# A two-block transformer stack on one core: the delta rule's triangular inverse by blocks of 16, and a reordered mixer

## What is computed

```
u = h @ w_in                       # q, k, v, z, b, a, sb_q, sb_k, sb_v, gate_a, gate_b
q, k, v = silu(conv4(q, k, v));  q, k = l2norm(q), l2norm(k)
beta = sigmoid(b);  g = -exp(a_log) * softplus(a + dt_bias)
o_a = gated_delta_rule(q, k, v, g, beta)          # 8 heads of 128
y_a = (rmsnorm(o_a) * silu(z)) @ w_branch_a
y_b = stick_breaking_attention(rmsnorm(sb_q), rmsnorm(sb_k), sb_v) @ w_branch_b
x  += (sigmoid(gate_a) * y_a + sigmoid(gate_b) * y_b) @ w_out
```

## Time and profile before

| | |
|---|---|
| median of 3 runs (lowest, highest) | 2795.54 us (2795.33, 2796.51) |
| the profiled execution's own time | 2795.47 us |
| span of its trace, first to last instruction | 2793.7 us |
| PE busy | 2540.9 us, 91% of the span |
| PE weight loads, beside it | 2360.2 us, 84% |
| DVE, ACT, POOL busy | 1538.1, 1404.1, 278.4 us |
| mean granted PE clock | 0.965 of full speed |
| DMA | 387.76 MB, mean 139 GB/s |

### The profile page before, as it was taken

The page is one execution under the profiler, slowest core; times in us unless marked ns, Lnnn a source line. Parts: engine busy times, 40 slices in busy tenths (PEclk is TensorE's granted clock), DMA queues, the critical chain, the costliest instruction groups (busy, mean ns, idle before and its releaser), DMA issues.

```text
span 2793.7 us, 46572 instructions
## 1 busy us (share of the span) xinstructions
PE 2540.9 (91%) x17917; PEld 2360.2 (84%) x17917; DVE 1538.1 (55%) x1836; ACT 1404.1 (50%) x1867; POOL 278.4 (10%) x469
## 2 busy tenths in 40 slices
PE   4999987899999899998689999989979998998998
PEld 4998876798899799887689889978878987887897
DVE  3554556445555555465554555547665544857554
ACT  3544766245545454476624545544554435455443
POOL 0000111730000000001272000000021001003000
PEclk9999998899999999999899999999999999999999
DMA  6554433014455455343301445643335564334553
GB/s 173 182 189 126 151 115 112 16 31 154 149 189 187 141 190 182 122 154 115 109 1 57 155 153 192 204 136 122 106 123 164 181 198 137 121 107 135 164 182 128
DMA packets 313158, 387.76 MB, mean 139 GB/s; under 512 B 10780, under 2 KB 288296, under 8 KB 313000
## 3 DMA queue, kind: packets, MB, share of 16 engines
q1 hardware_dynamic: 311664, 383.98, 42.5%
q10 hardware_dynamic: 1336, 1.67, 0.5%
HBM read 383.00 MB, written 2.62 MB: 138 GB/s over the span
## 4 chain that ended last, share of the span: by engine, by line
PE 69%; issue 9%; ACT 8%; DVE 7%; POOL 5%; DMA 1%; ACTq 0%; DVEq 0%; POOLq 0%; SPq 0%
PE bank L253 21%; PE bank L254 20%; PE bank L255 20%; ACT whi L239 4%; POOL arena L1218 3%; DVE wlo L245 2%; DMA raw<-in_ffn_w_in 1%; PE bank L333 1%; DVE arena L1760 1%; PE bank L611 1%; POOL arena L1203 1%; ACT arena L1657 1%; ACT arena L1639 0%; PE bank L936 0%; POOL arena L1208 0%
## 5 line engine op out<-in xcount | busy, mean ns | idle before, releaser
L245 DVE TENSOR_TENSOR wlo<-raw,whi 128x2048 fp32r<-128x2048 f32 x360 | 830.2, 2307 | 521.1 <-ACT whi L239 517.0
L253 PE MATMUL bank<-xhi,whi 128*128 128x256 f32 x3712 | 1070.3, 288 | 40.0 <-DVE arena L450 19.8
L254 PE MATMUL bank<-xlo,whi 128*128 128x256 f32 x3712 | 1056.0, 284 | 0.0
L255 PE MATMUL bank<-xhi,wlo 128*128 128x256 f32 x3712 | 1055.7, 284 | 0.0
L253 PEld LDWEIGHTS bank<-xhi,whi 128*128 128x128 f32 x3712 | 718.4, 194 | 55.7 <-issue 36.8
L239 ACT ACTIVATE whi<-raw 128x2048 fp32r<-128x2048 f32 x360 | 682.0, 1904 | 125.9 <-PE bank L255 101.5
L254 PEld LDWEIGHTS bank<-xlo,whi 128*128 128x128 f32 x3712 | 718.3, 193 | 5.3 <-issue 2.4
L255 PEld LDWEIGHTS bank<-xhi,wlo 128*128 128x128 f32 x3712 | 717.7, 193 | 0.0
L253 PE MATMUL bank<-whi,yhi 128*128 128x512 f32 x608 | 238.1, 392 | 9.3 <-DVE ylo L454 6.1
L254 PE MATMUL bank<-wlo,yhi 128*128 128x512 f32 x608 | 237.5, 391 | 0.0
L255 PE MATMUL bank<-whi,ylo 128*128 128x512 f32 x608 | 236.6, 389 | 0.0
(11 more groups left out here) (363 smaller groups left out, 3242.7 us busy)
## 6 DMA issues: line engine op xcount, KB each, us to landing
raw<-in_w_in SPq DMA_DIRECT2D x92, 1024.0 KB, 5.2
raw<-in_ffn_w_in SPq DMA_DIRECT2D x88, 1024.0 KB, 5.1
raw<-in_ffn_w_out SPq DMA_DIRECT2D x44, 1024.0 KB, 5.0
raw<-in_w_gate SPq DMA_DIRECT2D x32, 1024.0 KB, 5.4
raw<-in_w_up SPq DMA_DIRECT2D x32, 1024.0 KB, 5.4
raw<-in_w_down SPq DMA_DIRECT2D x32, 1024.0 KB, 5.1
raw<-in_w_branch_b SPq DMA_DIRECT2D x8, 1024.0 KB, 5.1
raw<-in_w_branch_a SPq DMA_DIRECT2D x8, 1024.0 KB, 5.1
```

The source lines that it names most:

```text
L245: e.tensor_tensor(wlo[s][:], raw[s][:], whi[s][:].bitcast(F32), ALU.subtract).then_inc(lo_done[s], 1)
L253: e.matmul(o, ahi, bhi, start=start, stop=False, skip_group_check=True)
L254: e.matmul(o, ahi, blo, start=False, stop=False, skip_group_check=True)
L255: return e.matmul(o, alo, bhi, start=False, stop=stop, skip_group_check=True)
```

## The change

The low four levels of the inverse (blocks of 1 to 16) are replaced. A mask "below" keeps the strictly lower part of the 128 diagonal blocks of 16x16 (16 matrices, 8 blocks each); 16 small matmuls gather them so that each partition holds one block; DVE inverts all 128 blocks at once by forward substitution along the free axis (`blocks_dve`, 29 dependent instructions on at most 240 elements, most on 56 or fewer), spreads the result, and 16 matmuls with two sets of copies and 16 more bring it back. Levels 4, 5 and 6 stay, with the mask moved from POOL ahead of the first product to DVE behind it, and with subtractions on packed halves. The gate and branch products of pairs 0 and 1 are issued inside the delta part, with the splits of units 31 to 34. All pairs alternate between two pairs of PSUM banks (4, 5 and 6, 7). The delta part no longer waits for the last silu, and POOL's spreading of g is gone (a broadcast operand of PE). In the loop over the 28 units silu's and the softplus' steps go ahead of the copy and of the taps, the attention heads take 4 turns and not 7, with two banks for the sums and two for the output, and b and a are made as 16 rows of 256 and then transposed (24 matmuls and 2 transposes). Two clearing products are gone.

```diff
+LOW = 4
+BLK = 1 << LOW
+    parts["below"] = (r // BLK == c // BLK) & (r > c)
+    parts["row_of"] = r % BLK == b[None, :]
+    parts["block_of"] = r % (P // BLK) == np.arange(P // BLK)[None, :]
-        HEAD_AT = (7, 9, 12, 14, 16, 18, 21, 23)
+        HEAD_AT = (6, 8, 11, 13, 15, 17, 20, 22)
@@ mix1_pe @@
-            norm_pe(e, j)
+            norm_pe(e, j, False)
-            mix1_delta_pe(e, l)
-            for n in range(PAIRS):
...
+            mix1_delta_pe(e, l, r0, u0)
+            for n in range(2, PAIRS):
+                pair_gate_pe(e, l, r0, u0, n)
+                pair_branch_pe(e, l, r0, u0, n)
+        def pair_gate_pe(e, l, r0, u0, n):
+            if n < 2:
+                e.wait_ge(*V["l_done"](l, 2 * n))
+            elif n < 4:
+                e.wait_ge(*V["od_r"](l, 2 * n - 4))
+            else:
+                e.wait_ge(*V["p_scaled"](l, n - 2))
+            feature_product(e, unit(r0, u0 + N1 + 2 * n), gate_bank(n), xhi, xlo)
@@ mix1_act, iteration n (the silu of n-1 ahead of the copy of n) @@
+                if head_at(n, 1) is not None:
+                    stick_softplus_act(e, l, head_at(n, 1))
+                if n - 1 in SILU:
+                    m = SILU.index(n - 1)
...
+                    e.activation(sg[m % 2], sg[m % 2], ACT.Ln, bias=one).then_inc(V["s_ln"].sem, 1)
+                if head_at(n, 3) is not None:
+                    stick_keep_act(e, l, head_at(n, 3))
@@ mix1_dve, iteration n (s_min of n-1 ahead of the taps of n) @@
+                if n - 1 in SILU:
+                    m = SILU.index(n - 1)
+                    e.wait_ge(*V["s_ln"](l, m))
+                    e.scalar_tensor_tensor(sg[m % 2], home(n - 1), 0.0, sg[m % 2], ALU.min, ALU.subtract)\
+                     .then_inc(V["s_min"].sem, 1)
@@ mix1_delta_pe @@
             e.wait_ge(*V["o_lo"](l, HEADS - 1))
-            e.wait_ge(*V["silu"](l, len(SILU) - 1))
             e.wait_ge(*V["normed"](l, len(NORM) - 1))
+            e.wait_ge(*V["pre_copied"](l, len(CONV) - 1))
...
+            pair_gate_pe(e, l, r0, u0, 0)
+            e.wait_ge(*V["m_ready"](l, GROUPS - 1))
+            e.wait_ge(*V["attn_done"](l, 0))
+            for c in range(BLK):
+                mm = e.matmul(bank[0][:, c * BLK:(c + 1) * BLK], M_blocks[:, :, c], const("row_of"), start=True, stop=True)
+            mm.then_inc(V["gathered"].sem, 1)
+            pair_branch_pe(e, l, r0, u0, 0)
+            pair_gate_pe(e, l, r0, u0, 1)
+            for b in range(4):
+                e.wait_ge(*V["spread"](l, b))
...
+                for i in range(4):
+                    mm = e.matmul(b4(b)[:, i, :], Ub[b][:, i, :], ident, start=True, stop=True)
+                mm.then_inc(V["scattered"].sem, 1)
+            pair_branch_pe(e, l, r0, u0, 1)
...
+            for g in range(GROUPS):
+                for i in range(4):
+                    mm = e.matmul(b4(g)[:, i, :], Tb[g][:, i, :], ident, start=True, stop=True)
+                mm.then_inc(V["tu_product"].sem, 1)
+            for s in range(LOW, LEVELS):
                 for g in range(GROUPS):
+                    e.wait_ge(*V["tu_done"](l, (s - LOW) * 4 + g))
+                    for i in range(4):
+                        mm = e.matmul(b4(g)[:, i, :], Lb[g][:, i, :], Ub[g][:, i, :], start=True, stop=True)
+                    mm.then_inc(V["m_product"].sem, 1)
+                for g in range(GROUPS):
+                    e.wait_ge(*V["w_kept"](l, (s - LOW) * 4 + g))
+                    for i in range(4):
+                        mm = e.matmul(halves(b4(g)[:, i, 0:64], s, False), Tb[g][:, i, :],
+                                      halves(Mb[g][:, i, :], s, True)[:, :, 1, :], start=True, stop=True)
...
@@ mix1_delta_act, behind the decay factors @@
+            split_hi(e, unit(r0, u0 + N1 + 3))
+            pair_gate_act(e, l, r0, u0, 0)
+            e.wait_ge(*V["gathered"](l))
+            e.activation(small_l, bank[0][:, 0:256], ACT.Copy).then_inc(V["l_compact"].sem, 1)
...
@@ mix1_delta_dve @@
                 up.then_inc(V["l_done"].sem, 1)
+            split_lo(e, unit(r0, u0 + N1 + 3))
+            for g in range(GROUPS):
                 e.wait_ge(*V["a_mask"](l, g))
                 e.wait_ge(*V["qk"](l, g))
                 e.tensor_tensor(flat(Ab[g]), bank[g][:], flat(Ab[g]), ALU.mult).then_inc(V["attn_done"].sem, 1)
+            pair_min_dve(e, l, 0)
+            blocks_dve(e, l)
+            pair_scaled_dve(e, l, r0, u0, 0)
+            split_lo(e, unit(r0, u0 + N1 + 4))
+            pair_min_dve(e, l, 1)
+            for b in (0, 1):
+                e.wait_ge(*V["scattered"](l, b))
+                e.tensor_copy(T_blocks[:, :, 4 * b:4 * b + 4], b4(b).rearrange("p c k -> p k c"))\
+                 .then_inc(V["t_kept_v"].sem, 1)
+            pair_scaled_dve(e, l, r0, u0, 1)
+            for g in range(GROUPS):
+                e.wait_ge(*V["tu_product"](l, g))
+                e.tensor_copy(flat(Ub[g]), bank[g][:]).then_inc(V["tu_done"].sem, 1)
+            for s in range(LOW, LEVELS):
+                mask = const(f"level{s}").unsqueeze(1).to_broadcast([P, 4, P])
+                for g in range(GROUPS):
+                    e.wait_ge(*V["m_product"](l, (s - LOW) * 4 + g))
+                    e.tensor_tensor(Mb[g], b4(g), mask, ALU.mult).then_inc(V["w_kept"].sem, 1)
+                for g in range(GROUPS):
+                    e.wait_ge(*V["tu_product"](l, (s - LOW) * 4 + 4 + g))
+                    if s < LEVELS - 1:
+                        t = pairs(Tb[g], s)[:, :, :, 0, :]
+                        e.tensor_tensor(t, t, packed(b4(4 + g), s), ALU.subtract)
+                    u = pairs(Ub[g], s)[:, :, :, 1, :]
+                    e.tensor_tensor(u, u, packed(b4(g), s), ALU.subtract).then_inc(V["tu_done"].sem, 1)
+                if s < LEVELS - 1:
+                    split_lo(e, unit(r0, u0 + N1 + 1 + s))
+        def blocks_dve(e, l):
...
+            e.tensor_tensor(small_t, const("eye"), small_l, ALU.subtract).then_inc(V["t_first"].sem, 1)
+            e.wait_ge(*V["t_first"](l))
+            for j in range(1, BLK - 1):
...
+                e.tensor_tensor(o, L[:, j:j + 1, j + 1:BLK].to_broadcast(shape), Tc[:, 0:j, j:j + 1].to_broadcast(shape),
+                                ALU.mult).then_inc(V["t_outer"].sem, 1)
+                e.wait_ge(*V["t_outer"](l, j - 1))
+                e.tensor_tensor(Tc[:, 0:j, j + 1:BLK], Tc[:, 0:j, j + 1:BLK], o, ALU.subtract).then_inc(V["t_step"].sem, 1)
```

More of the change, by code:

```diff
@@ L602, in mix1_pe @@
                         feature_product(e, unit(r0, u0 + n), bank[n % 2], xhi, xlo)
-                if n == 2:
+                if n == 1:
+                    e.wait_ge(*V["ba_copied"](l))
+                    e.sem_inc(tensor_waited)
+                    for t in range(TT):
+                        mm = e.transpose(bank[4][:, t * 16:(t + 1) * 16], ba_turn[:, t * P:(t + 1) * P], ident[0:16, 0:16])
+                    mm.then_inc(V["ba_turned"].sem, 1)
+                if n == 4:
                     e.wait_ge(*V["g_done"](l))
@@ L641, in kept_unit, with gate_bank, branch_out_bank @@
+        def gate_bank(n):
+            return bank[4 + n % 2 * 2]
+        def branch_out_bank(n):
+            return bank[5 + n % 2 * 2]
         def kept_unit(e, l, n):
@@ L672, in mix1_act @@
                     split_hi(e, unit(r0, u0 + n + 2))
-                if n == 3:
+                if n == 0:
+                    e.wait_ge(*V["ba_product"](l))
+                    e.activation(ba_turn, bank[4][0:16, 0:T], ACT.Copy).then_inc(V["ba_copied"].sem, 1)
+                if head_at(n, 1) is not None:
+                    stick_softplus_act(e, l, head_at(n, 1))
+                if n - 1 in SILU:
+                    m = SILU.index(n - 1)
+                    if n - 1 in CONV:
+                        e.wait_ge(*V["tap"](l, CONV.index(n - 1) * 4 + 3))
+                    else:
+                        e.wait_ge(*V["kept"](l, PLAIN.index(n - 1)))
+                    if m >= 2:
+                        e.wait_ge(*V["silu"](l, m - 2))
+                    e.activation(sg[m % 2], home(n - 1), ACT.Abs).then_inc(V["s_abs"].sem, 1)
+                    e.wait_ge(*V["s_abs"](l, m))
+                    e.activation(sg[m % 2], sg[m % 2], ACT.Exp, scale=-1.0).then_inc(V["s_exp"].sem, 1)
+                    e.wait_ge(*V["s_exp"](l, m))
+                    e.activation(sg[m % 2], sg[m % 2], ACT.Ln, bias=one).then_inc(V["s_ln"].sem, 1)
+                if head_at(n, 3) is not None:
+                    stick_keep_act(e, l, head_at(n, 3))
+                if n == 5:
                     small_act_2(e, l)
@@ L963, in stick_keep_act @@
             e.wait_ge(*V["o_product"](l, g))
-            e.activation(yhi[:, g, :], bank[7][:, 0:256], ACT.Copy).then_inc(V["o_hi"].sem, 1)
+            e.activation(yhi[:, g, :], bank[6 + g % 2][:, 0:256], ACT.Copy).then_inc(V["o_hi"].sem, 1)
         def stick_softplus_dve(e, l, h):
@@ L1090, in flat, with pairs, packed @@
```

(8 more changed lines are left out.)

330 lines of the change are left out of this document (155 added, 175 removed).

## The result

The changed kernel takes 2666.9 us (median of 4 runs, 2666.75 to 2667.26), the kernel before beside it 2796.0: the ratio is 0.954, with a 95% interval of 0.952 to 0.956. The forecast was 2662 us in a range of 2630 to 2715. The profiled execution after took 2666.87 us with a span of 2664.9, which is 128.8 less than the span before.

A forecast was written before the change was run, and what follows sets the result against it. PE, busy 91% of the span, bounds the kernel, so gains come from its idle or slow time or removed work. 2.9 + 10 + 20.2 + 33.5 = 66.6 us a layer, twice 133, takes 2795.5 to 2662 us; range 2630 to 2715.

The forecast's parts named there:

- b and a: 2.9 us: Products for b and a in each layer's mixer: 24 fewer at 0.12 us each save 2.9 us.
- The loop: 10 us: Loop over 28 units: gain 10 us a layer, ends 0 and 30; units 17 to 27 take 77 plus 2, against 89.6.
- Rival 1: In the loop, ACT takes the ring's place, so no gain there: 2682 us; chance 0.15.
- the ring: ACT and DVE waiting on each other in the loop's late units: 9.33 us a turn where PE needs 5.76 to 8.
- From unit 27 to gate 2: 112.3 us: Delta part, from the end of unit 27 to gate 2: 112.3 us instead of 132.5, saving 20.2 a layer.
- The costly order: DVE's low split of unit 31 ahead of the attention products: about 9 us of DVE waiting, PE idle 5.
- the lower end: Levels 4 to 6: if 64 columns cost half, DVE's 8.4 us would bind, 6.6 us less in all.
- Rival 2: The clock falls within the levels, whose 28.4 us double at half clock: 2719 us; chance 0.10.
- The pairs: 69.1 us: Six pairs behind the delta part, with alternating banks, at PE's rate: 69.1 us instead of 102.6, saving 33.5.
- rival 3: The pairs don't quicken, because of DMA or ACT's splits: 77 us instead of 69, 2678 us; chance 0.08.
- rival 4: PE at half clock from the end of unit 27 to the last pair, slower than before: 2935 us; chance 0.02.
- rival 5: More is won in the loop, all 32.9 us of waits and half clock, not 13: 2622 us; chance 0.08.

The follow-up runs named there:

- experiment 6: The changed kernel with b and a in their old form, 48 products with 16 moving columns instead of 24 with 256, no turning back: 2681.9 us, ratio 0.959.
- experiment 7: The changed kernel with DVE's minimum with the softplus of unit n-1 put back behind the taps of unit n: 2691.1 us, ratio 0.963.
- experiment 1: The changed kernel with DVE's low split of unit 31 behind the block inversion, not ahead of the attention products: 2657.0 us, ratio 0.951.
- experiment 2: The changed kernel with 43 more products of 256 columns, unused by the output, between gate 0 and the gather: 2665.0 us, ratio 0.954.
- experiment 10: The changed kernel without block inversion: T and U start as identities and all seven levels run: 2715.9 us, ratio 0.972.
- experiment 9: The changed kernel with DVE's chain of 29 small steps made twice in a row: 2673.4 us, ratio 0.957.
- experiment 3: The changed kernel with three other product forms (strided or side-by-side weights, 16 or 128 moving columns) ahead of the gather, 60 wide products before each: 2747.1 us, one run.
- experiment 4: The changed kernel with POOL writing the masked L so that each gather product's 128 columns lie side by side: 2670.5 us, ratio 0.955.
- experiment 5: The changed kernel with both DVE's low split of unit 31 behind the blocks and the gather's columns side by side: 2646.7 us, ratio 0.946.

## Why the prediction was right, point by point

*What bounds the kernel.* Right: the gain came from PE's idle time, its half clock and work taken away, in the places named.

*b and a: 2.9 us.* Too small. Up to the end of the unit behind them, 16.35 us became 10.45, so 5.9. The step counted products at 0.12 us and left out that the old 48 had run at 0.21, at a clock of 0.50, which the mean of 0.93 in the earlier trace rows hides; experiment 6 gives 7.5. The clearing products were hidden, as said: from the last pair to the output products it is 2.5 us before and after.

*The loop: 10 us.* Units 18 to 27 took 79.4 to 79.6 us (77 + 2 forecast, 89.6 before), the units ahead of them gained 1.5. PE waited 2.8 us at most for a query and 3.3 for a mask, where the walk had 3.6 and 2.2. Rival 1 (ACT takes the ring's place) is out. But the reason given, the ring cut, carries only 4 of the 10 in these units (experiment 7), and 5 more behind them, which the prediction had counted under the gap.

*From unit 27 to gate 2: 112.3 us.* It was 115.1. Against the schedule:

| step, us from the end of unit 27 | forecast | measured |
|---|---|---|
| first row of g | 2.1 | 3.2 |
| head of ACT's part begins | 9.8 | 11.4 |
| first group of L | 19.3 | 20.5 |
| gate 0 ends | 27.2 | 26.5 |
| gather begins, ends | 32.3, 37.5 | 31.8, 38.7 |
| branch 0 ends | 43.3 | 46.5 |
| products for U begin | 58.4 | 61.6 |
| level 6 ends | 92.0 | 94.3 |
| gate 2 begins | 112.3 | 115.1 |

Two terms were off. The 2 us of half clock were put on gate 0, which had none; they came in branch 0, 7.8 us instead of 5.8, and with the gather, not with PE's thin use ahead of it (experiments 1, 2 and 10). And the gather, taken at 5.2 between 0.4 and 7.1, lay at its upper end. The upper bound had the right size and half of the reason: it was worked out as half clock, and the gather did run at 0.50, but the runs showed 0.21 us a record at full clock too, from the stride. The costly order stood where it was said, PE's wait was 5.17 us, and it is worth 4.4 to 5 us a layer (experiment 1).

*Steps, scatter, copies.* Hidden as said: 28 steps in 6.6 us, from 493.2 to 499.8, 6 us ahead of the scatter, with 4.4 us of slack (experiment 9).

*Levels.* 10.67, 11.0 and 7.43 us (10.7, 11.45 and 7.85 forecast). 64 moving columns cost as much as 128, 0.89 us per group of four, so the lower end (-6.6 us) is out. Rival 2 is out: the clock was 1.00 in the levels. The Trainium skill ("TensorE: Matmul & The Clock Gate", "HAM oscillation — how this bites in real kernels") has idle gaps between bursts bring the clock down; the trace agrees for the gap of 5.2 us (0.50 in the five microseconds behind), while in the levels no such gap was left. The fall within the gather, with PE busy and no gap (experiment 2), is not of the kind that this section tells of.

*The pairs: 69.1 us.* 69.7, at a clock of 1.00; the bank's wait is gone, and DMA with 152 GB/s did not bind. The eight before took 102.2 us, not 102.6. Rivals 3, 4 and 5 are out by the total. One argument against rival 4 was false all the same: cold stretches did not always end once PE was busy, since the clock of the kernel before fell to 0.50 during its unbroken work on b and a (experiment 6).

*The sum.* 67.6 us in the first layer for 66.6, but with terms of +3.0 (b and a), +1.7 (loop), -2.8 (delta part) and -1.0 (pairs), which cancel: that the sum came so close is partly luck. The second layer gave 62.0: after, the two mixers are alike (429.9 and 431.4), but before the second was already 4.1 us shorter. That the layers are not twins was left out, and is most of the 5 us between 2662 and 2667.

## What to carry to other kernels

An engine's list is a queue: a step that waits for something not needed yet holds up all behind it (here the low split of unit 31, done at 484.5 us for a product at 509.2); move it behind the work that others wait for. Two slow causes that overlap hide each other: from gate 0 to level 4, over the two layers, taking away the stride alone gave nothing and taking away the wait alone 9 us, both together 15. Measure such things in the stretch itself as well, and in every repeat of it that the trace has: the totals moved by up to 12 us from one execution to the next, and it was the second layer that showed the clock falling without the stride. And where a stretch is slow at half clock, ask first how long one record takes in a stretch at full clock, before the clock gets the blame.

## What the hardware showed that was not expected

- fp32 weights with 64 bytes from one column to the next: 0.21 to 0.22 us a record, 0.106 to 0.113 side by side, at a granted clock of 1.00, with 16 or 128 moving columns (experiment 3). At a clock of 0.50 the form side by side takes 0.21 as well (experiment 4).
- A granted clock that falls while PE is busy without a gap, each time with products of 16 moving columns: from 0.99 or 1.00 to 0.50 within the strided gather of 6.7 us (experiments 1, 2 and 3), behind or within the same products with weights side by side (experiment 5 in both layers, experiment 3 in one of two), and in the fp32r products for b and a of the second layer of the kernel before. In 7.0 us of the same strided weights with 128 moving columns it stayed at 1.00 in both layers (experiment 3). In the other direction, the 48 products with 16 moving columns went by at 0.50 for all of their 10 us after a cold start, where with 24 of 256 the clock was back 4 to 5 us behind their start (experiment 6). What decides is open.
- Dependent small steps on DVE start 0.21 to 0.25 us apart, from 14 to 56 elements, though the longest record is 0.22 us.
- POOL writes with a stride of 512 bytes at the price of a dense write, 1.26 us for 512 columns (experiment 4).
